# A hybrid decoder step on one core: the attention stage laid out anew (eight value buffers, queries kept in SBUF, head norm in line, scores one block ahead)

## What is computed

```python
q = rope((h @ w_q).reshape(B, S, N_HEADS, 2, HEAD_DIM), pos) * (HEAD_DIM ** -0.5)
lam = jnp.exp(jnp.sum(lp[0] * lp[1])) - jnp.exp(jnp.sum(lp[2] * lp[3])) + lam_init
s = jnp.einsum('bqhmd,bkhmd->bhmqk', qb, k_all).astype(jnp.float32)
s = jnp.where(k_pos[None, :] <= qpb[:, None], s, -jnp.inf)
p = jax.nn.softmax(s, axis=-1)
att = p[:, :, 0] - lam * p[:, :, 1]
o = jnp.einsum('bhqk,bkhe->bqhe', att, v_all)
o = rms_norm(o, subln_g) * (1.0 - lam_init)
return o.reshape(B, S, N_HEADS * V_DIM) @ w_o
```

## Time and profile before

| | us |
|---|---|
| median of 3 runs | 2704.74 (2703.04 to 2707.0) |
| the profiled execution | 2704.4 |
| its span, first to last instruction | 2702.5 |
| mean granted TensorE clock in it | 0.93 |

### The profile page before, as it was taken

The page is one execution under the profiler, slowest core; times in us unless marked ns, Lnnn a source line. Parts: engine busy times, 40 slices in busy tenths (PEclk is TensorE's granted clock), DMA queues, the critical chain, the costliest instruction groups (busy, mean ns, idle before and its releaser), DMA issues. The chain is left out here.

```text
span 2702.5 us, 42179 instructions
## 1 busy us (share of the span) xinstructions
PE 2451.0 (91%) x18388; PEld 2275.9 (84%) x18388; DVE 987.5 (37%) x1569; ACT 792.5 (29%) x998; POOL 242.7 (9%) x181
## 2 busy tenths in 40 slices
PE   4999999898899999979899999975777788999996
PEld 3999999797799999979899999974344487999996
DVE  4222232676522223253423222253444354232324
ACT  4212212475421221243421221243222243212123
POOL 1100101100110010110210000010000012101010
PEclk8999999898899999989899999987777688999998
DMA  7333331122232333323233333325877311222221
GB/s 307 141 141 141 140 138 63 54 79 74 110 142 85 148 141 139 124 74 114 85 138 145 129 144 136 125 72 210 308 276 272 110 47 63 79 83 90 79 71 61
DMA packets 66938, 343.11 MB, mean 127 GB/s; under 512 B 9410, under 2 KB 11586, under 8 KB 37314
## 3 DMA queue, kind: packets, MB, share of 16 engines
q1 hardware_dynamic: 62658, 333.33, 33.2%
q10 hardware_dynamic: 4096, 7.08, 0.7%
HBM read 330.80 MB, written 9.58 MB: 126 GB/s over the span
## 5 line engine op out<-in xcount | busy, mean ns | idle before, releaser
L478 PE MATMUL ps<-hh_hi,w_hi 128*128 128x288 f32 x3456 | 1002.6, 303 | 75.1 <-POOL hh_lo L1439 70.8
L478 PE MATMUL ps<-hh_lo,w_hi 128*128 128x288 f32 x3456 | 988.8, 299 | 0.0
L481 PE MATMUL ps<-hh_hi,w_lo 128*128 128x288 f32 x3456 | 752.1, 299 | 0.0
L478 PEld LDWEIGHTS ps<-hh_hi,w_hi 128*128 128x128 f32 x3456 | 660.2, 191 | 100.9 <-issue 57.9
L478 PEld LDWEIGHTS ps<-hh_lo,w_hi 128*128 128x128 f32 x3456 | 662.0, 192 | 0.2
L481 PEld LDWEIGHTS ps<-hh_hi,w_lo 128*128 128x128 f32 x3456 | 564.6, 192 | 0.0
L1066 DVE TENSOR_TENSOR w_lo<-raw,w_hi 128x2048 fp32r<-128x2048 f32 x164 | 376.1, 2293 | 324.8 <-ACT w_hi L698 314.7
L478 PE MATMUL ps<-h_hi,w_hi 128*128 128x288 f32 x1664 | 475.6, 299 | 20.5 <-POOL h_lo L1439 20.5
L478 PE MATMUL ps<-h_lo,w_hi 128*128 128x288 f32 x1664 | 472.3, 297 | 0.0
L698 ACT ACTIVATE w_hi<-raw 128x2048 fp32r<-128x2048 f32 x164 | 312.1, 1903 | 345.6 <-PE ps L481 318.0
L481 PE MATMUL ps<-h_hi,w_lo 128*128 128x288 f32 x1664 | 358.8, 296 | 0.0
(11 more groups left out here) (179 smaller groups left out, 1439.1 us busy)
## 6 DMA issues: line engine op xcount, KB each, us to landing
raw<-in_w_gu SPq DMA_DIRECT2D x88, 1024.0 KB, 4.8
ada<-in_ada_w SPq DMA_DIRECT2D x76, 1024.0 KB, 10.7
raw<-in_w_d SPq DMA_DIRECT2D x32, 1024.0 KB, 4.8
kr<-in_k_cache SPq DMA_DIRECT2D x64, 512.0 KB, 5.9
vr<-in_v_cache SPq DMA_DIRECT2D x64, 512.0 KB, 5.5
raw<-in_w_d SPq DMA_DIRECT2D x16, 768.0 KB, 4.4
raw<-in_w_in SPq DMA_DIRECT2D x8, 1024.0 KB, 4.9
raw<-in_w_kv SPq DMA_DIRECT2D x8, 1024.0 KB, 4.8
```

The lines of the kernel that those rows point to most:

```text
L478: pe.matmul(ps[:, 2 * s + n, 0:TH], whi, r[:, k, TH * n:TH * n + TH], start=(k == 0 and r is rhs_hi), stop=False)
L481: mm = pe.matmul(ps[:, 2 * s + n, 0:TH], wlo, rhs_hi[:, k, TH * n:TH * n + TH], start=False, stop=(k == k_tiles - 1))
```

## The change

It touches the q stage, the attention stage and the first unit of w_o.

- **Layout.** The attention tiles are laid so that keys, queries and query scratch don't lie over what the q stage uses. There are eight value buffers; `vr4` to `vr7` lie over the odd weight unit (`w_hi1`, `w_lo1`). So no weight unit is split into the odd pair until the last value page is used (a wait on `v_used` in the `down` stage on ScalarE and VectorE).
- **Queries.** The rope sum goes to `oT` in SBUF, head by head; there is no `qT`, no store and no query load. A head's output overwrites its queries later. `rope` gets its tiles as arguments.
- **First keys.** Between the loads of units 2 and 3 of w_q, SP loads both key groups of sequence 0 and `ks`, `vs`. w_o's first two units are loaded in round 2 and the first is split in round 3, not in the q stage.
- **Scores ahead.** TensorE issues the scores of block t + 1 ahead of the transposes of block t; VectorE's maximum follows the scaling of the block before. The maximum is negated in the reduction.
- **Head norm in line.** Head n - 1 is normed in round n: square, logarithm and exponential on ScalarE, one column sum on TensorE, scaling on VectorE; its copy to `h_hi` and low part come in round 7 (POOL's for heads 6 and 7 after the last value product). ScalarE loads once a table with both functions. The samples are normed together at the end.
- **w_o's first tile** is computed by column halves: first the 288 columns without samples, head by head, then the others.

```diff
+        laid("odd_unit", None, ("w_hi1", [P, 8, 256], F32R), ("w_lo1", [P, 8, 256], F32R))
+        laid("odd_pages", None, *[(f"vr{i}", [P, N_HEADS * P], F32) for i in range(4, N_PAGES)])
+        laid("q_out", 4 * hh, ("oT", [P, N_HEADS, T], F32), ("qbd", [P, N_HEADS * 144], F32),
+             ("ks", [P, N_HEADS, S_TOK], F32), ("q_swapped", [P, T], F32), ("q_a", [P, T], F32), ("q_b", [P, T], F32))
+        laid("pages", 2 * hh, ("kr0", [P, 4, N_HEADS, PAGE], F32), ("kr1", [P, 4, N_HEADS, PAGE], F32),
              ("vs", [S_TOK, N_HEADS, P], F32))
-        laid("att_prompt", att0, ("qh0", [P, SEQ], F32), ("qh1", [P, SEQ], F32), ("kh0", [P, SEQ], F32),
-             ("kh1", [P, SEQ], F32), ("vh0", [P, 4, P], F32), ("vh1", [P, 4, P], F32), ("pp0", [P, 2, SEQ], F32),
-             ("pp1", [P, 2, SEQ], F32), ("oT", [P, N_HEADS, T], F32), ("qbd", [P, N_HEADS * 144], F32),
-             ("probs", [P, PAST_LEN + S_TOK], F32))
+        laid("heads", 0, *[(f"vr{i}", [P, N_HEADS * P], F32) for i in range(4)],
+             ("kh0", [P, SEQ], F32), ("kh1", [P, SEQ], F32), ("vh0", [P, 4, P], F32), ("vh1", [P, 4, P], F32),
+             ("pp0", [P, 2, SEQ], F32), ("pp1", [P, 2, SEQ], F32))
+        laid("weights", 4 * hh + N_HEADS * (T + 144 + S_TOK), ("probs", [P, PAST_LEN + S_TOK], F32))
...
+            def v_load(b, p):
+                page = page_of(b, p, v_cache)
+                if b:
+                    sp.wait_ge(sems["v_used"], N_PAGES * (b - 1) + p + 1)
+                sp.dma_start(vr[p][:, :], v_cache[bass.ds(page, 1)].rearrange("o p n -> p (o n)"))\
+                    .then_inc(sems[f"v_full{p}"], 16)
+            def head_load(h):
+                j = h % 2
+                if h >= 2:
+                    sp.wait_ge(sems["pv_done"], 4 * (h - 1) + CREDITS["pv_done"])
+                sp.dma_start(kh[j][:, :], kT_out[h, :, 0:SEQ]).then_inc(sems[f"kh_full{j}"], 16)
+                sp.dma_start(vh[j][:, :, :], v_prompt[h]).then_inc(sems[f"vh_full{j}"], 16)
...
+                            if s["kind"] == "q" and (i, j) == (1, 0):
+                                sp.wait_ge(sems["w_done"], u0 + CREDITS["w_done"])
+                                for g in range(2):
+                                    k_load(0, g)
+                                sp.dma_start(ks[:, :, :], kT_out[:, :, SEQ:T].rearrange("h p s -> p h s"))\
+                                    .then_inc(sems["s_small"], 16)
+                                sp.dma_start(vs[:, :, :], v_sample.rearrange("h s e -> s h e"))\
+                                    .then_inc(sems["s_small"], 16)
...
+                    for h in range(2):
+                        head_load(h)
+                    for p in range(N_PAGES):
+                        v_load(0, p)
                     for g in range(2):
                         k_load(1, g)
...
+                    for n in range(DEC_BATCH):
+                        if n + 2 < DEC_BATCH:
+                            for g in range(2):
+                                k_load(n + 2, g)
+                        if n == 2:
+                            for j in range(2):
+                                unit_load(w_o, j, u0 + j, j)
+                        if n + 1 < DEC_BATCH:
+                            for p in range(N_PAGES):
+                                v_load(n + 1, p)
+                        if n + 2 < N_HEADS:
+                            head_load(n + 2)
...
+            def products_by_half(j, first):
+                for n in range(2):
+                    if n == 1:
+                        pe.wait_ge(sems["ss_lo"], 1)
+                    for k in range(KT):
+                        if n == 0:
+                            pe.wait_ge(sems["h_lo"], first + k + 1 + CREDITS["h_lo"])
+                        whi, wlo = w_hi[j][:, k, 0:P], w_lo[j][:, k, 0:P]
+                        for w, r in ((whi, h_hi), (whi, h_lo), (wlo, h_hi)):
+                            mm = pe.matmul(ps[:, n, 0:TH], w, r[:, k, TH * n:TH * n + TH],
+                                           start=(k == 0 and w is whi and r is h_hi), stop=(k == KT - 1 and w is wlo))
+                mm.then_inc(sems["out0_full"], 1)
...
+                            mm = pe.matmul(ps[:, 4 + m, 0:n], oT[rows, t // 4, P * i:P * i + P], kh[j][rows, 0:n],
...
+                            if h:
+                                pe.wait_ge(sems["so_ln"], h)
...
+                    def scores_ahead(t):
+                        n, i = t // 4, t % 4
+                        if i == 0:
+                            pe.wait_ge(sems[f"kh_full{n % 2}"], 16 * (n // 2) + 16)
+                        scores(i, n % 2, t)
+                    def head_sums(h):
+                        pe.wait_ge(sems["o_evac"], h + 1 + CREDITS["o_evac"])
+                        pe.wait_ge(sems["so_sq"], h + 1)
+                        pe.matmul(ps[:, 7, :], ones, o_sq, start=True, stop=True).then_inc(sems["so_sum"], 1)
...
+                    def round_(n, j, more):
                         for i in range(4):
                             t = 4 * n + i
-                            scores(i, j, t)
                             if i == 0 and more:
                                 page_scores(n + 1, 0)
+                            if i == 0 and n:
+                                head_sums(n - 1)
                             if i == 1:
                                 if more:
                                     page_scores(n + 1, 1)
...
                             if i >= 2:
                                 page_outputs(n, i - 2)
+                            if t + 1 < 4 * N_HEADS:
+                                scores_ahead(t + 1)
                             turn(n, i, t, more)
                             weigh(n, i, j, t)
...
+                    head_sums(N_HEADS - 1)
+                    pe.wait_ge(sems["ss_sq"], 1)
+                    pe.matmul(ps[:, 4, :], ones, sq_s.rearrange("p h s -> p (h s)"), start=True, stop=True)\
+                        .then_inc(sems["ss_sum"], 1)
...
+                    def head_gain(h):
+                        act.wait_ge(sems["o_evac"], h + 1 + CREDITS["o_evac"])
+                        act.wait_ge(sems["so_sum"], h)
+                        act.activation(o_sq, oT[:, h, 0:SEQ], ACT.Square).then_inc(sems["so_sq"], 1)
+                        act.wait_ge(sems["so_sum"], h + 1)
+                        act.wait_ge(sems["so_n"], h)
+                        act.activation(o_rs, ps[:, 7, :], ACT.Ln, scale=1.0 / P, bias=eps_o)\
+                           .then_inc(sems["so_ln"], 1)
+                        act.wait_ge(sems["so_ln"], h + 1)
+                        act.activation(o_rs, o_rs, ACT.Exp, scale=-0.5).then_inc(sems["so_rs"], 1)
+                    def head_hi(h):
+                        act.wait_ge(sems["kg_done"], 2 * DEC_BATCH + CREDITS["kg_done"])
+                        act.wait_ge(sems["so_n"], h + 1)
+                        act.activation(h_hi[:, h, 0:SEQ], oT[:, h, 0:SEQ], ACT.Copy).then_inc(sems["h_hi"], 1)
                     def round_(n, more):
                         for i in range(4):
                             exps(i, 4 * n + i)
+                            if i == 0 and n:
+                                head_gain(n - 1)
                             if i == 3:
...
+                            if i == 0 and n == 3:
+                                split_unit((u0 // 2, u0), 0)
+                            if not more:
+                                for h in ((), (0, 1, 2), (3, 4), (5, 6))[i]:
+                                    head_hi(h)
+                    act.preload_act_table_set("natural_log_exp_and_others")
...
-                        dve.tensor_reduce(mx, ps[:, 4:6, 0:n], AXX, ALU.max).then_inc(sems["max_ready"], 1)
-                        dve.wait_ge(sems["max_ready"], t + 1)
                         dve.wait_ge(sems["p_ready"], t + CREDITS["p_ready"])
-                        dve.tensor_scalar(nmx, mx, -1.0, None, ALU.mult).then_inc(sems["nmx_ready"], 1)
+                        dve.tensor_reduce(nmx, ps[:, 4:6, 0:n], AXX, ALU.max, negate=True)\
+                           .then_inc(sems["nmx_ready"], 1)
...
+                    def head_norm(h):
+                        dve.wait_ge(sems["so_rs"], h + 1)
+                        dve.wait_ge(sems["o_evac"], h + 1 + CREDITS["o_evac"])
+                        dve.scalar_tensor_tensor(oT[:, h, 0:SEQ], oT[:, h, 0:SEQ], gain_o, o_rs, ALU.mult,
+                                                 ALU.mult).then_inc(sems["so_n"], 1)
                     def round_(n, more):
                         for i in range(4):
-                            maximum(i, 4 * n + i)
                             if i == 1 and more:
                                 sample_mask(n + 1)
                             differ(i, 4 * n + i)
-                            if i == 1 and more:
-                                sample_max(n + 1)
+                            if i == 1:
```

(17 more changed lines are left out.)

241 lines of the change are left out of this document (96 added, 145 removed).

## The result

| | before | after |
|---|---|---|
| median of 4 runs | 2705.87 (2703.04 to 2714.61) | 2562.53 (2556.71 to 2563.45) |
| the profiled execution | 2704.4 | 2563.45 |
| its span | 2702.5 | 2561.2 |
| mean granted TensorE clock | 0.93 | 0.959 |

What follows compares the result with a forecast made beforehand. In the attention rounds it took one chain of waits, and the TensorE clock they lowered, as the bound. Start 22, rounds 39.4, round 7 11, tail 19.7 and tables 1.3 made 93.4 off 2704.4: 2611.0, range 2585 to 2648.

Steps and rivals of the forecast that it cites:

- So only the stretch from 1855 to about 2192 can move.: Whole kernel: everything outside this stretch is dense weight matmuls that the change doesn't touch, so gains come only from there.
- Which c? I take 0.90.: Rounds 1 to 6: mean TensorE clock c rises from 0.72 to 0.90, giving 26.8 us a round, 39.4 us off.
- rival (a): Rounds, start and round 7: the clock stays up, rounds of 24.6, about 18 us more off, 2593; chance 0.20.
- 20.3 + 22.3 x (1 - c).: Matmul time of one attention round in us at mean clock c: 20.3 at 2.4 GHz, 31.4 at 1.2 GHz.
- The idle time of a round, 3.2: TensorE idle per round: 2.3 us for the copy, 0.6 for the head norm, 0.3 for the transposes.
- The start, 22: Start of attention: first page product 11.9 us earlier, block 1's keys 19.4, rest of round 0 2.6; 22 us off.
- Round 7 and the tail, 11 and 19.7: Round 7 falls from 34.0 to 23 us; first output tile comes 13 us after the last value product, for 32.7.
- Tables, 1.3: ScalarE behind attention: one table for logarithm and exponential saves the 1.283 us reload at L730.
- (b): Rounds: waits go but the clock stays at 0.72, rounds of 30.8, 24 us dearer, 2643; chance 0.20.
- (c): ScalarE in each round: tables reload for the logarithm and back, 21 us dearer, 2632; chance 0.04.
- (d): Attention: transfers through one queue decide below 221 GB/s; at 200, 32 us late, 2736, slower; chance 0.04.

Runs made afterwards that it cites:

- The filled and unfilled waits: Changed kernel with a useless 2000-column VectorE reduction in step 3 of each round: unfilled 2589.3; with 18 useless TensorE transposes in that wait, 2576.88.
- the run with the short gap: Changed kernel with a useless 960-column VectorE reduction in step 3 of each round, ahead of the scaling the transposes wait for: 2572.32, ratio 0.9509.

## Why the prediction was right in direction and wrong in size

- **"So only the stretch from 1855 to about 2192 can move."** This step failed. It followed the instructions of the other stages, which are the same, and not the addresses that the layout gives to their operands. The units' 21 us of gain, nearly half of the miss, were not in the sum at all; the run with the addresses of after in the kernel before shows that they alone make them.
- **"Which c? I take 0.90."** This step failed too. The clock was 1.00 in rounds 1 to 6: 2.2 us a round, 13 in all. The argument of the earlier trace rows was right in kind: the clock fell behind 2.65 us of idling, and no wait in rounds 1 to 6 is above 0.71, but for the 1.17 at their very end. The filled and unfilled waits show that idling does it. Wrong was the weight given to the short waits in a row in step 2 (0.38 and 0.58 us, with full speed behind them); a clock that stays up is rival (a), which had 0.20.
- **"20.3 + 22.3 x (1 - c)."** This term was mis-sized at its full-speed end. A full round is 19.9 busy with the head sum of 1.1 in it, so 18.7 (18.75 in the run without the norm in the rounds), 1.6 less than 20.3: 9 us over six rounds. The line went through two windows at 0.77 and 0.70, and c = 1 lies far beyond both. From 18.7 the two points give 28 to 29 us per unit of clock instead of 22.3.
- **The idle time of a round, 3.2:** measured 2.9. The copy's waits are 14.7 us over six rounds (2.3 a round forecast, 2.45 measured), the transposes' 2.3 (0.3 and 0.4); these hold the norm's 0.6, which came as forecast (2.27 idle a round without the norm). With the two points above: 6 x (2.2 + 1.6 + 0.3) = 24.6, for the 24.0 by which the six rounds missed.
- **The start, 22:** measured 23.2. First page product: 11.6 us earlier than in before, counted from the end of the query products (17.59 of waiting to 5.98), 11.9 forecast; block 1's keys 17.2 earlier for 19.4; the rest of round 0 gave 6.1 for 2.6. So the total is right by luck: 2.2 short in one term, 3.5 over in the other. Without the loads in the query stage 13 us of it are gone. No weight unit came late: TensorE is busy 45.17 us in the window from 1793.00, which is all of it up to its last query product at 1838.17.
- **Round 7 and the tail, 11 and 19.7:** 10.6 and 21.6. The last value product ends at 2045.04 and the first tile at 2056.28, 11.2 us for the 13 that I took, at the good end of the bounds, since the clock stayed at 1.00. Round 7 kept the low-clock piece that the prediction gave all rounds; the window's clock is 0.92. In step 2 the products behind a wait of 1.39 us take 1.65 us for 0.94:

```profile
2036.66 0.55 PE L594 MATMUL ps<-cst,nt 128*128 128x128 f32 x3 [1.39 <-DVE nt L1400]
2037.79 1.65 PE L606 MATMUL ps<-nt,vh 128*128 128x128 f32 x6 [0.58 <-ACT nt L946]
```

- **Tables, 1.3:** the two loads are gone (7 to 6 at each of the two lines), and the idle time ahead of the next norm's first product falls from 7.19 to 5.92. Yet from w_o's second tile to the first up unit the kernel before takes 72.4 us and the one after 72.6. The clock gave it back: the column sums take 2.29 us for 1.63, and the stretch from the last wait for the activations' low part to the first up unit, before and then after, is 1.5 us longer at a clock of 0.77 for 1.00:

```profile
2261.74:2270.67 8.93, 8.55 (x62) 8.32 (x63) 2.29 (x2) 3.62 (x3) 1.39 (x1) 1.00 0.34 119
2124.91:2135.33 10.42, 10.41 (x62) 10.42 (x63) 2.29 (x1) 3.63 (x3) 1.39 (x1) 0.77 0.28 101
```

Why the clock differs there was not tried.

- **The rivals.** (a) was what happened in the rounds, and still 30 us short. (b) fell: the clock rose when the long waits went. Its stretch at 0.50 with 11.55 of 12.60 us busy had begun with such a wait, of 2.03 us:

```profile
2018.58 1.12 PE L575 MATMUL ps<-cst,nt 128*128 128x128 f32 x4 [2.03 <-DVE nt L1354]
```

(c) shows nowhere: no table load in the rounds. (d) fell: it needed under 221 GB/s, and the six rounds moved 376; TensorE never waits for a page after round 0, and a third less to move changed nothing. At 406 to 419 GB/s in the run with the norm at the end, rounds of 21.0 us went below even the 22.2 that the prediction worked out for the transfers.

## What to carry to other kernels

Where the layout moves, the stages that it doesn't touch move too: compare addresses as well as instructions, and keep a term for it. A long wait on TensorE (2.0 to 3.1 us here) often has two prices, itself and the half-speed stretch behind it, so taking away the last one in a round brings more than its length, and a second cause of such a wait (here the buffers) eats much of what removing the first one brings. For a rate at the other clock, add up rows that ran at that clock; a line through two near-by mixtures is no measurement.

## What the runs showed of the hardware that was not expected

- The same 96 matmuls at the same granted clock of 1.00 take 12.48, 12.64, 12.77 or 12.80 us, and moving the tiles in SBUF alone changes it. All even units of a feed-forward take the same time, and all odd ones; in two placements the last feed-forward has another value (12.48) than the earlier ones (12.64).
- The same wait can be followed by either clock. One of 2.04 us was followed by 1.2 GHz in four rounds of six and by full speed in two. A wait of 1.52 us was followed by a fall in the kernel before, one of 1.54 us was not in the run with the scores put back, where one of 2.45 us was not either. That of 1.39 us in round 7 was followed by a fall in the kernel after and not in the run with the short gap. The waits of 0.96 us of that run were not followed by one. What decides is open.
- 2.18 us of nothing but transposes, in the place of a wait behind which it had fallen, kept the clock at 1.00.
- The queue that brings the pages moved 417 GB/s over a whole round of 23.3 us, and 419 over one of 21.0.
